# A hybrid decoder layer on one core: routing and experts in one program, the first round outside the loop, expert rows added to x by DMA

## The reference, cut to what matters

```python
x = x + concatenate([o_da, o_rw]) @ w_out[l]
h = rmsnorm(x, ffn_norm_w[l])
x = x + moe_ffn(h, router_w, router_b, mlp1_w, mlp1_b, mlp2_w, mlp2_b)
return rmsnorm(x, final_norm_w)

def moe_ffn(h, ...):
    logits = xf @ router_w + router_b            # 512 x 32
    top_val, top_idx = lax.top_k(logits, 4)
    gates = softmax(top_val)
    # for each expert e and the tokens that chose it:
    gu = xb @ mlp1_w[e] + mlp1_b[e]              # 1024 x 2048 weights
    gate, up = gu[..., ::2], gu[..., 1::2]
    gate, up = minimum(gate, 7), clip(up, -7, 7)
    act = (up + 1) * gate * sigmoid(1.702 * gate)
    y = act @ mlp2_w[e] + mlp2_b[e]              # 1024 x 1024 weights
    out[token] += y * gate_of_token
```

## Time and profile before

| | us |
|---|---|
| median of 3 runs | 1749.18 (1747.82 to 1750.51) |
| the profiled execution | 1748.68 |
| its span, first to last instruction | 1746.8 |
| front block | 0 to 438 |
| output_and_route | 438 to 518.9 |
| experts up to the first product with weights | 519 to 534.4 |
| turns 0 and 1 | 534.4 to 596.8 |
| 30 turns of the loop, 36.05 each | 596.8 to 1678 |
| last down pieces | to 1701.8 |
| the end | to 1746.8 |

### The profile page before, as it was taken

The page is one execution under the profiler, slowest core; times in us unless marked ns, Lnnn a source line. Parts: engine busy times, 40 slices in busy tenths (PEclk is TensorE's granted clock), DMA queues, the critical chain, the costliest instruction groups (busy, mean ns, idle before and its releaser), DMA issues.

```text
span 1746.8 us, 28600 instructions
## 1 busy us (share of the span) xinstructions
...
## 2 busy tenths in 40 slices
...
GB/s 185 242 38 25 26 37 38 26 1 2 208 169 287 241 363 370 361 357 367 358 381 372 349 375 369 371 368 347 368 363 368 352 359 368 364 359 361 358 207 248
DMA packets 100824, 467.62 MB, mean 268 GB/s; under 512 B 12734, under 2 KB 39374, under 8 KB 51488
## 3 DMA queue, kind: packets, MB, share of 16 engines
...
...
## 4 chain that ended last, share of the span: by engine, by line
PE 65%; DVE 1%; issue 1%; DMA 1%; ACT 1%; SPq 0%; DVEq 0%; POOL 0%; POOLq 0%; ACTq 0%
PE psum L1775 27%; PE psum L1778 13%; PE psum L1796 13%; PE psum L1801 6%; PE psum L1767 2%; PE psum L1757 2%; PE psum L1787 1%; PE psum L1748 1%; DMA o_t<-expert_rows 1%; ACT w_pieces_hi L1491 0%; DMA expert_rows<-ys,this_i 0%; DMA xg<-h_rows,gath_i 0%; DVE xl L1614 0%; DVE w_pieces_lo L1597 0%; SPq L1416 0%
## 5 line engine op out<-in xcount | busy, mean ns | idle before, releaser
L1597 DVE TENSOR_TENSOR w_pieces_lo<-w_pieces,w_pieces_hi 128x2048 fp32r<-128x2048 f32 x384 | 870.7, 2287 | 91.0 <-ACT w_pieces_hi L1491 91.0
L1491 ACT ACTIVATE w_pieces_hi<-w_pieces 128x2048 fp32r<-128x2048 f32 x384 | 736.7, 1919 | 296.7 <-PE psum L1778 225.2
L1775 PE MATMUL psum<-w_pieces_hi,xh 128*128 128x512 f32 x1024 | 293.6, 409 | 1.1 <-DVE xl L1614 1.1
L1775 PE MATMUL psum<-w_pieces_hi,xl 128*128 128x512 f32 x1024 | 277.5, 393 | 0.0
L1778 PE MATMUL psum<-w_pieces_lo,xh 128*128 128x512 f32 x1024 | 277.3, 393 | 0.0
L1775 PEld LDWEIGHTS psum<-w_pieces_hi,xl 128*128 128x128 f32 x1024 | 193.7, 189 | 43.4
L1778 PEld LDWEIGHTS psum<-w_pieces_lo,xh 128*128 128x128 f32 x1024 | 193.4, 189 | 43.1
L1775 PEld LDWEIGHTS psum<-w_pieces_hi,xh 128*128 128x128 f32 x1024 | 182.4, 190 | 42.9 <-issue 12.0
L1457 POOL DMA_INDIRECT expert_rows<-ys,this_i x31 | 156.8, 5059 | 269.0 <-ACT ys L1511 269.0
L1796 PE MATMUL psum<-w_pieces_hi,ah 128*128 128x512 f32 x512 | 160.7, 395 | 0.0
L1796 PE MATMUL psum<-w_pieces_hi,al 128*128 128x512 f32 x512 | 158.2, 390 | 0.0
...
## 6 DMA issues: line engine op xcount, KB each, us to landing
...
w_raw<-in_w_in SPq DMA_DIRECT2D x26, 512.0 KB, 3.8
...
w_pieces<-expert_rows SPq DMA_DIRECT2D x12, 512.0 KB, 13.5
w_pieces<-in_w_out SPq DMA_DIRECT2D x8, 512.0 KB, 9.7
chunk_work<-in_x SPq DMA_DIRECT2D x4, 512.0 KB, 5.5
x<-in_x SPq DMA_DIRECT2D x4, 512.0 KB, 13.8
h_rows<-w_pieces POOLq DMA_DIRECT2D x4, 512.0 KB, 2.9
```

What stands on the lines that cost most here:

```text
L1491: nc.scalar.activation(hi[:, p % RING], raw[:, raw_slot(b, p)].rearrange("p r n -> p (r n)"), ACT.Copy).then_inc(s_hi, 1)
L1597: nc.vector.tensor_tensor(lo[:, p % RING], raw[:, raw_slot(b, p)].rearrange("p r n -> p (r n)"), hi[:, p % RING].bitcast(F32), ALU.subtrac ...
L1775: nc.tensor.matmul(bank(c), a[:, k, :], hi[:, p % RING, c * 512:(c + 1) * 512], start=False, stop=False)
```

## The change

What it does, part by part:

- **One block.** `output_and_route` returns five functions, one for each engine, and the block of `experts` calls them first. The barrier between the two blocks is gone. The first round's `select`, `numbers` (formerly half of `indices`) and `number_sum` are written inside the routing.
- **First round outside the loop.** `rounds` calls `run(0)` and then loops over the rounds 1 to 3. `run(0)` and the later rounds no longer wait at their end for the stored output; that wait stands at the very end of SP's program, and in `again` at the start of a later round.
- **Routing chain.** The transposes take x after the projection, not the normalised h2 (L1297 of the changed kernel); the norm weights are multiplied into the router weights, and 1/rms is applied to the logits (L1223). Tokens are the rows of the product now, so the logits need not be transposed back. The transposes of tile 2 and the logits of tiles 0 and 1 stand inside the projection of tile 3. The fourth largest is found with `max` and `match_replace`; the mask is the comparison of the logits before and after. Which of its token's four rows an expert gets is a running count (`tensor_tensor_scan`). The ranks come from 5 products with fp32r operands in place of 14 with float32. The four gate columns are summed after the two index columns (`number_sum` in two calls).
- **Loads of the first pieces.** Piece 0 is loaded as soon as the biases are split; pieces 1 and 2 when h_rows is stored and the logits are made; pieces 3 to 5 when the first gather has landed.
- **Turns 0 and 1.** The second half of `turn_x` goes to bank 6, so that it need not wait for the first; the first products wait for the first half of `xl` alone. In turn 1 the sigmoid stands before the fourth piece's ACT copy, and `activate` right behind the fourth piece on DVE, ahead of the second half of `xl`.
- **The end.** `SCATTERED` is 30: the last two experts stay on the chip, so `choose` has twice the products. In place of the 16 loads, POOL issues 16 accumulating DMAs (`accum_op=add`) that add rows of expert_rows to x, four for each tile, each waiting for the one before it on the same tile. DVE makes one addition for each tile.

```diff
 def output_and_route(...):
...
         for p in range(RAW):
+            if p == 1:
+                sp.wait_ge(s_store, 16 * NT)
+                sp.wait_ge(s_log, NT)
+            if p == 3:
+                sp.wait_ge(g["s_gath"], 16)
             sp.dma_start(raw[:, p].rearrange("p r n -> p (r n)"), gate_up_rows(d, 0, p)).then_inc(g["s_raw"][p], 16)
...
+        def choose(t):
+            dve.wait_ge(s_log, t + 1)
+            chain(nc.vector.scalar_tensor_tensor(lg[:, t, :], bank(t, 0, EXPERTS), stat[:, 32 + t:33 + t], rb[:], ALU.mult, ALU.add))
+            chain(nc.vector.max(top8[:, t, :], lg[:, t, :]))
+            chain(nc.vector.tensor_scalar(r1[:, t:t + 1], top8[:, t, 0:1], -1.0, None, ALU.mult))
+            chain(nc.vector.memset(top8[:, t, 4:8], 3e38))
+            nc.vector.match_replace(rest[:, t, :], top8[:, t, :], lg[:, t, :], -3e38)
+
...
+        choose(0)
+        choose(1)
+        add_x(3)
+        dve.wait_ge(s_turn3, 1)
+        nc.vector.tensor_copy(x2t[:, 0:4, 3 * P:4 * P], bank(6).rearrange("p (k c) -> p k c", c=P)).then_inc(s_xt3, 1)
+        choose(2)
+        rstd(3)
+        normed(3)
+        choose(3)
...
+        nc.vector.tensor_tensor(rank[:, :, 0:EXPERTS], hidden[:], ranks, ALU.add)
...
+        g["select"](0, 0)
         dve.wait_ge(s_exp, 1)
...
         for k in range(KT):
             project_out((3,), k)
...
+            if k == 2:
+                turn(2)
+            if k == 3:
+                pe.wait_ge(s_xt, 2)
+                logits(0, range(KT))
+            if k == 4:
+                logits(1, range(KT))
+        pe.wait_ge(s_xt, 3)
+        logits(2, range(5))
+        turn(3)
+        logits(2, range(5, KT))
+        pe.wait_ge(s_xt3, 2)
+        logits(3, range(KT))
...
+        g["number_sum"](0, 0, 2)
+        pe.wait_ge(s_info, 2)
+        g["number_sum"](0, 2, 4)
...
+    def rounds(eng, run, again=None):
+        run(0)
+        with eng.Fori(1, ROUNDS) as r:
             flag = eng.value_load(flags[0:1, bass.ds(r, 1)])
             with eng.If(flag == 1):
+                if again:
+                    again(r)
                 run(r)
...
-            sp.wait_ge(s_scat, (r * SCATTERED + SCATTERED) * 16)
-            sp.sem_inc(s_part, 1)
-            for t in LAST_ROWS:
-                if t < 3:
-                    sp.wait_ge(s_lo, r * STREAM + (STREAM + 2 * t + 2))
-                for k in range(4):
-                    sp.dma_start(row(t, k), rows_v[t, :, k, :]).then_inc(s_row[t][k], 16)
...
-            pool.wait_ge(s_tx, (r * TURNS + EXPERTS) * 2 + 2)
+            pool.wait_ge(s_tx, (r * TURNS + EXPERTS) * 2 + 3)
             pool.sem_inc(s_part, 1)
             nc.gpsimd.dma_start(fw[:], d["final_norm_w"].to_broadcast([P, D])).then_inc(s_fw, 16)
-            pool.wait_ge(s_hot, r * NT + NT)
+            for k in range(4):
+                for t in LAST_ROWS:
+                    if k:
+                        pool.wait_ge(s_row[t], (r * 4 + k) * 16)
+                        pool.sem_inc(s_part, 1)
+                    nc.gpsimd.dma_start(x[:, t, :], rows_v[t, :, k, :], accum_op=ALU.add).then_inc(s_row[t], 16)
...
             for p in range(DOWN, PIECES):
-                split(r, 1, p)
                 if p == 7:
                     sigmoid(r, 0, 0, PIECES - 1)
+                split(r, 1, p)
...
             for n, t in enumerate(LAST_ROWS):
-                f = final[t][:]
-                for k in range(2):
-                    dve.wait_ge(s_row[t][k], r * 16 + 16)
-                nc.vector.tensor_tensor(f, row(t, 0), row(t, 1), ALU.add).then_inc(s_add, 1)
...
                 dve.wait_ge(s_hot, r * NT + (n + 1))
+                dve.wait_ge(s_row[t], r * 64 + 64)
+                nc.vector.tensor_tensor(x[:, t, :], psum[:, last_banks[t]:last_banks[t] + 2, :].rearrange("p b n -> p (b n)"), x[:, t, :],
+                                        ALU.add).then_inc(s_add, 1)
                 if n:
                     finish(n - 1)
...
                 down_piece(r, b + 1, p, 0)
+                if p == 0:
+                    pe.wait_ge(s_sel31, r + 1)
+                    turn_choice(2)
```

447 lines of the change are left out of this document (247 added, 200 removed).

## The result

The changed kernel takes 1723.26 us (median of 4 runs, 1721.08 to 1725.52), the kernel before 1749.85 us on the same chip (4 runs, 1747.82 to 1750.78): ratio 0.985, 95% interval 0.9831 to 0.9868. The forecast was 1726, in a range of 1709 to 1744. A second measurement of the same kernel, on another chip, gave 1724.39 us (5 runs) and again 0.985 (0.9834 to 0.9865).

A forecast was written before the change was run, and what follows sets the result against it. PE was taken to bound the unchanged loop, and chains through several engines the places around it. Gains of 14.1 (routing), 0 (turns 0 and 1) and 8.8 (end) from 1748.68 gave 1725.8, with 0.5 us for the median 1726; range 1709 to 1744.

The forecast's parts named there:

- Routing: Up to the first weight product: last addition of x 4.8 us later, but that product near 520.3, a gain of 14.1 us.
- Turns 0 and 1: First product of turn 1 4.3 us later, offset by 2.6 of wait and 1.7 of half clock: 0 change.
- The loop: From 600 to 1682 us, PE busy throughout at full clock: 30 turns of 36.05 us unchanged.
- The end: Behind the last weight product: accumulations replace 16 additions and the program's end shortens, a gain of 8.8 us.
- u: Time of one accumulating transfer at the end, taken as 2.52 us, twice a plain load's 1.26.
- The choice that releases the accumulations is turned at 1685.2: At the end: this sets the accumulations' release, with data flowing from about 1687 after five issues.
- the front: Everything ahead of the loop, routing and turns 0 and 1: a gain of 14.1 + 0 us.
- Full rate: Rival at the end: an accumulation takes only a plain load's 1.26 us, total 1712 us; chance 0.18.
- The price of a lone transfer: Rival at the end: each accumulation costs 5.2 us and they bound it, total 1769 us; chance 0.09.
- slower: Outcome of a kernel slower than before, deciding at u = 3.95 us; chance 0.09.
- The front gives part back: Rival: gather lands 3 us late and turn 1's 4.3 us come without their return, total 1733 us; chance 0.14.

The follow-up runs named there:

- experiment 5: Changed kernel with turn 1 in its old order (sigmoid behind the split of piece 7, activate behind that of piece 8): 1722.83 us.
- Experiment 3: Changed kernel, but norm weights and accumulations also wait for ACT's copy of the first turned choice: 1728.9 us.
- experiment 4: Kernel before, with 16 accumulating transfers in place of the plain loads and 16 of 20 additions, scatter of expert 30 kept: 1763.56 us.
- experiment 2: Changed kernel with the same 16 transfers as plain copies into x, without the adding: 1713.0 us.

## Why the prediction was right, and where its sum was not

**Routing: right, with its details.** Forecast: the addition 4.8 us later, measured 4.6. Chosen mask complete at about 503.4, table at 507.3, first weight product at 520.3; measured in the first profile, which stands 1.3 us later as a whole (480.29 against 479.03 at the first transposition): 504.7, 508.2, 520.68. The gain is 14.1 forecast and 13.7 from one absolute position to the other; counted from the first transposition of x it is 15.0. Both rests of the first pieces and then xl set the start, as forecast; the gather was ready just ahead of ACT. The ten other profiles with the code of the changed kernel up to here put the product 40.4 to 41.9 us behind the first transposition (before 55.4), so 13.5 to 15.0 us is the gain. The parts of this change (one block, the shorter chain, the order of the loads) were not taken back one at a time, so what each is worth stays the forecast's estimate.

**Turns 0 and 1: right, to 0.4 us in a typical profile.** From the first weight product to the end of turn 1 it is 62.4 us before (534.42 to 596.80) and on average 62.8 in the eight profiles with the lower clock at that product; the forecast was no change. The parts, from experiment 5: start 4.2 us later (forecast 4.3), wait before the transposed activations gone (2.8, forecast 2.6). The piece behind that wait was 1.1 us faster, not 1.7, the transposition 0.4, and the first piece of the turn was in this pair 1.05 us longer at the lower clock, which the sum did not hold. The first profile has 60.6 us instead, by its high clock in turn 0, a gain of chance that is not in a typical run.

**The loop: right.** Nothing of it changed, and both kernels are PE-bound at full clock there; the 30 turns are the same in both traces, 36.05 us each (1679.99 - 598.44 and 1664.52 - 582.91 for 30, from clipping to clipping).

**The end: right about the transfer, wrong about its start.** The rate is the step on which the forecast rested, u = 2.52 us, twice the time of a plain load. Measured 2.47 to 2.50, and 1.25 for the same transfer without the adding. The trace moves some 211 GB/s of rows where plain loads move 410 to 430. The Trainium skill, Collectives: The Full Stack, section "The bandwidth ceiling: the fold count and why AG ≠ RS ≠ AR", says that the reducing step of a collective runs at half the rate of the copying one, because its add reads two sources. The trace agrees in the rate, 211 GB/s against 410 to 430; that the two reads are the reason no run here shows. Windows of the profile after, with the columns as above:

```profile
1655.00:1660.00 5.00, 5.00 (x26) 4.12 (x25) 4.16 (x4) 3.26 (x2) 0.00 (x0) 1.00 0.99 378
1670.00:1680.00 10.00, 10.00 (x52) 8.39 (x51) 8.90 (x6) 8.30 (x8) 2.55 (x3) 1.00 1.06 211
```

The DMA share (the column before the last) is at 0.99 with weight pieces and at 1.06 with accumulations, while the GB/s fall from 378 to 211. The engines are as busy, with half of the result.

The step that failed is "The choice that releases the accumulations is turned at 1685.2". I took this from ACT's copy of the turned choice. POOL waits for a count that PE raises with an instruction of its own, written behind the transposition of the choice. It is not raised when the transposition is done either. In the kernel before it is L1854, in the changed one L1947, and the transposition there is L1892:

```profile
L1854 PEldq EVENT_SEMAPHORE  x1: 51/51/51, 1677.9 to 1677.9; - x1
...
L1947 PEldq EVENT_SEMAPHORE  x1: 51/51/51, 1662.4 to 1662.4; - x1
...
1665.54 0.60 PE L1892 MATMUL psum<-cst,sel 128*128 128x128 f32 x4
```

The count is raised 3.1 us before the transposition starts (1662.4, 1665.54; before: 1677.9, 1681.07), and 3.1 to 3.2 us before it in every other profile as well. So the trace of before had the right date, 1677.9, in the row of the semaphore. In the profile after, POOL starts at 1663.05, which is 1678.5 on the clock of before: 6.7 us early against the forecast. Experiment 3 puts the start back to ACT's copy and loses 6.3 us.

The end missed by less than 6.7 us, and that is partly luck. From POOL's first issue to the end of the last scaling the forecast had 49.0 us (1685.2 to 1734.2), and it took 52.3 (1663.05 to 1715.35). Where no weight pieces run beside the transfers it is 50.6 (experiment 3) and 50.1 (experiment 4), so some 2 us are the price of running beside them (up to 14.8 us to landing, median of all 9.5), a term that the forecast left out. The two errors leave 3.4 us at the last scaling. Behind it the forecast had 3.8 us and the profile has 4.35. So the end's gain is 11.6 and not 8.8 us, a miss of 2.8.

**The sum.** Forecast 14.1 + 0 + 8.8 = 22.9 us. The first profile has 15.5 + 11.6 = 27.1 (positions 1679.99 to 1664.52, then B); by the medians it is 26.6, and 25.7 by the second measurement. With the typical A of 1169.5 the sum is 1188.1 - 1169.5 - 4.6 + 11.6 = 25.6. So the front, 14.0 against 14.1, holds, and the miss of 2.7 us is the end's.

**The rivals.** Full rate fell with the spacing of 2.50 us, and experiment 2 shows what it would have been: 1713, forecast 1712. The price of a lone transfer, 5.2 us, never occurred. But the side of "slower" was nearer than its chance of 0.09 says: it hung not on u alone but also on the start, and experiment 4 shows the accumulations as a loss of 15.9 us where they start behind the scatter. "The front gives part back" described two real mechanisms, but neither cost what it said: the gather is slowed by 3 to 5 us only with five pieces before it, and even then the total does not show it; turn 1 takes 22.6 us on average against 23.1 before.
